# Value projections interleaved by weight chunk, squares and a norm row issued later, and a cross-attention regrouped through DRAM

## The chip, the cores and the metric

The kernel runs on one core of a Trainium2 chip. The metric is device time in microseconds (us) of one execution; the median of several executions counts. One further execution is recorded by the hardware profiler, and all rows below come from that one.

## The reference

Two small transformer stacks run one after the other on a sequence of 512 tokens with 1024 features, in float32. What matters here:

```python
# first_block, two layers; per layer
u = einsum('bsd,dc->bsc', rmsnorm(x), w_in)            # all projections
ya = forgetting_attention(qa, ka, va, log_f)           # 4 heads of 64
yb = dilated_mixture_attention(rope(qb), rope(kb), vb) # 6 heads of 64
yc = banded_attention(rope(qc), rope(kc), vc, 127, sinks)
x = x + (sigmoid(ga)*(ya*silu(za)) @ w_br_a + ... ) @ w_out

# second_block, two layers
h = h + even_mixer(...)       # layer 0: a = softmax(q1 k1) - lam * softmax(q2 k2), then a @ v,
                              # an rms norm of each head, and a pooling branch
h = h + cross_attention(...)  # q from h, k and v from a 256-token memory, 4 heads of 256, softmax, no mask
h = h + sq_relu_mlp(...)
# layer 1: a short convolution instead of the even mixer, then the same two
```

## The kernel before

Every matrix product of float32 operands is made of three TensorE products: each operand is split into a rounded high part and the rest, and high·high, high·low and low·high are added in one PSUM bank. Weights come in chunks of 128 x 1024 from DRAM into `raw` (4 slots). For each chunk ScalarE writes the high part `whi` (`round_hi`, 4 slots) and VectorE the rest `wlo` (`rest_lo`, 3 slots). `ahead(i)` issues these when the program comes to chunk i: high parts up to chunk i+3, rests up to i+2, each only if the slot's former user is done. `fetch(j + 4)` follows `rest_lo(j)` on the queue of SyncE (SP).

`gemm_fm` makes a product with features on the partitions (8 steps of 3 matmuls of 512 columns, lines 378 to 380). `gemm_tm` makes a value projection with tokens on the partitions: two chunks `w[0]` and `w[1]` hold the 1024 input features, and for each of two token tiles of one bank all 8 feature blocks k are added (lines 404 to 406, 256 columns each); it yields after every second k. `w[1]` holds k = 4 to 7.

Each engine runs its instructions in the order of the program. The program is written as Python generators: `drive(main, fill, num, den)` takes one step of the attention (`main`), then num/den steps of projections (`fill`), so that TensorE has projections to do while VectorE and ScalarE work at the softmax. `later(f, n)` puts f off to the n-th `flush()`; `flush` is called after each yield of an attention and at each end of a product (`finish`). `stage` puts three steps of a norm's column and row onto ticks (k steps) of the products that follow, and products that end before the last step is out hold their evacuation back (`held_back`).

In the first block, attention goes by units (a pair of heads with one or two query tiles). After the softmax its probabilities have to be transposed. Here (`by_dma=True`) ScalarE writes them, scaled, in blocks of 32 columns into `blocks`; `send_away` writes that to DRAM (`far`), and reads it back with the 32-row groups exchanged (4 DMAs, `grouped`); `turn_near` transposes 32 x 32 blocks on VectorE (`turned`). Step i holds `values` of unit i-3, `turn_near` of i-2, `scores` of i, a yield, `norm` and `send_away` of i, a yield.

The even mixer of the second block uses the same function without DMAs. `norm` takes the reciprocal of the sums, scales the first map by a `tensor_scalar` on VectorE, and adds the second map with a `scalar_tensor_tensor` (line 184). `turn` transposes on TensorE (line 705) and copies to `PTb` on ScalarE; `values` (line 729) reads that. After the last unit of a head, `head_done` copies the head out of PSUM on VectorE (line 1433), squares it on ScalarE and, three flushes later, sums the squares (`stats`).

The cross-attention (`cross`) runs in both layers. Step i holds `norm` of unit i-1 (a `tensor_tensor` over 512 columns), `scores` of i (line 1505, 8 matmuls), a yield, `values` of i-2 (line 1555), `turn` of i-1 (4 transposes of 128 x 128 on TensorE, line 1531, and a copy on ScalarE), a yield. In layer 0, five steps of projections stand at each yield, among them the keys and values of layer 1.

Of the kernel before, what the change touches and what calls it, by code (L numbers as in the profile page):

```python
# [7 lines left out]
ACT = mybir.ActivationFunctionType  # L8
ALU = mybir.AluOpType
# [133 lines left out]
def lay_out(nc, A, plan, T):  # L143
# [42 lines left out]
    def ts(o, a, s1, s2, f, g=ALU.bypass):  # L186
        return lambda e: e.tensor_scalar(o, a, s1, s2, f, g)  # L187
# [202 lines left out]
    def gemm_tm(src, chunks, evac, nt=4):  # L390

        w = [Weight(c) for c in chunks]
        for t0 in range(0, nt, 2):
            bank, free = G.take()
            o = None
            for t in (t0, t0 + 1):
                for k in range(8):
                    v, b = w[k // 4], 2 * (k % 4)
                    wh, wl = v.hi(b, 2), v.lo(b, 2)
                    xh, xl = src.hi[:, k, 128 * t:128 * t + 128], src.lo[:, k, 128 * t:128 * t + 128]  # L400

# [162 lines left out]
        return make  # L564


    def attention(units, done_pair, late_values=False, by_dma=False):

        st = {}
# [49 lines left out]
        def norm(u):  # L619
# [6 lines left out]
            if by_dma:  # L626
# [10 lines left out]
                    TB.give(t, last[-1])  # L637
                    o += last
                STT.give(s, o[-1])
                u["far"] = far, o  # L640
                return
            for j, (t, _) in enumerate(u["T"]):
                c = 12 + 2 * j
# [13 lines left out]
        def send_away(u):  # L657

            n = 2 * (u["cols"] // 128)
            src, o = u["far"]  # L660
            w, k = moved[0] % 2, moved[0] // 2
            moved[0] += 1
            far = A["far"][w][:, :, 0:32 * n]

            def write():
                u["out"] = Q.dma(SP, lambda e: e.dma_start(far.rearrange("j p c -> p j c"),
                                                           src[:, 0:128 * n].rearrange("p (j c) -> p j c", j=4)),
                                 T["s_t"][w], 16 * (k + 1), o, back[w])
                blocks.give(src, u["out"])
                later(rest)  # L670

            def rest():
                dst, dfree = grouped.take()
                for j in range(4):
                    landed = Q.dma(SP, lambda e, j=j: e.dma_start(
                        dst[32 * j:32 * j + 32, 0:128 * n].rearrange("p (i c) -> p i c", i=4),
                        far[j].rearrange("(i a) c -> a i c", i=4)),
                        T["s_u"][w], 16 * (4 * k + j + 1), u["out"], dfree)
                back[w] = landed
                u["near"] = dst, landed  # L680

            later(write)

        def turn_near(u):

            n = 2 * (u["cols"] // 128)
            src, landed = u["near"]
            dst, dfree = turned.take()
            o = op(DV, lambda e: e.transpose(dst[:, 0:128 * n].rearrange("p (k i b) -> p k i b", i=4, b=32),
                                             src[:, 0:128 * n].rearrange("p (i k b) -> p k i b", i=4, b=32)),  # L690
                   landed, dfree)
            grouped.give(src, o)
            u["PT"] = [o]
            u["cut"] = [lambda k, h=h: dst[:, u["cols"] * h + k:u["cols"] * h + k + 128] for h in range(2)]
            u["held"] = dst

        def turn(u):
            cols = u["cols"]
# [49 lines left out]
        if by_dma:  # L748
            for i in range(n + 3):
# [212 lines left out]
    for l in range(2):  # L962
# [167 lines left out]
            assert len(grouped.idle) == 1  # L1130
            drain()

        phase("forget", tok, 2, qA, kA, vA, [0, 1], [0, 1], gens_B(tokB), 90, 15, M[:, 4:6, :])
        phase("mix", tokB, 3, qB, kB, vB, [2, 3, 4], [2, 3, 4], gens_C(tokC), 138, 21, QKV[:, 4:6, :])
        phase("sink", tokC, 3, qC, kC, vC, [5, 0, 1], [0, 1, 2], gens_D(), 112, 15, QKV[:, 6:8, :])
# [295 lines left out]
    def head_done(u, banks, p):  # L1431
        h = u["pair"]
        o = op(DV, lambda e: e.tensor_copy(qE[:, h, :], banks[0]), p)
        t, sq = tmp_act_square(qE[:, h, :], o)

        def rest():
            hs[h] = stats(t, sq, out=lp[:, 136 + 4 * h:140 + 4 * h], inv=1.0 / 128)
            TMP.give(t, hs[h])

        later(rest, 3)  # L1440
        return [o]

    def even_main():
# [31 lines left out]

    run(mixed("ab_w_out", 0, halves(0), 1.0, "xa0", P1))
    row_end()

    def cross(l, gname):
        qX = E3[:, 0:8, :]  # L1480
# [37 lines left out]
        def norm(u):  # L1518
            t, s = u["t"], u["s"]
            r = op(DV, lambda e: e.reciprocal(s[:, 6:8], s[:, 4:6]), u["exp"])  # L1520
            u["P"] = op(DV, mult(both(t), both(t), s[:, 6:8].unsqueeze(2).broadcast_to([128, 2, 256])), r)
            STT.give(s, u["P"])

# [19 lines left out]

        def values(u):
            h, n = u["head"], u["half"]
            pt, ready = u["PT"]
# [13 lines left out]
            PTS.give(pt, p)  # L1560
            u["over"] = True
            if n == 1:
                for d in range(2):
# [5 lines left out]

        def main():  # L1570
            n = len(un)
            for i in range(n + 2):
                if 1 <= i <= n:
                    norm(un[i - 1])
# [6 lines left out]
                if 1 <= i <= n:  # L1581
                    turn(un[i - 1])
                yield

        def nxt(m, o):
            norm_tile(m, o, gname, P0, sqa)
# [144 lines left out]
    flush()  # L1731
    run(mixed("conv_w_out", 0, halves(0), 1.0, "xa1", P1))
    row_end()
    cross(1, "mlp1")

    end = [{"sum": None, "gained": []} for _ in range(2)]
# [270 lines left out]
```

How the kernel before makes its waits and increments, by code:

```python
    def dma(self, eng, fn, sem, val, *deps):  # L94
        self.op(eng, lambda e: fn(e).then_inc(sem, 16), *deps)
        return Landed(sem, val)
# [9 lines left out]
    def play(self, eng, e):  # L106
        seen = {}
        for o in self.of[eng]:
            need = {}
            for d in o.deps:
                v = need.get(id(d.sem), (0, None))[0]
                need[id(d.sem)] = (max(v, d.val), d.sem)
            for k, (v, s) in need.items():
                if seen.get(k, 0) < v:
                    e.wait_ge(s, v)
                    seen[k] = v
            ins = o.fn(e)
            if o.sig:
                ins.then_inc(o.sem, 1)
# [23 lines left out]
def lay_out(nc, A, plan, T):  # L143
# [1657 lines left out]
                o = send(0, *((0, 3), (3, 3), (6, 2))[m - 3])  # L1801
                if m == 5:
                    SB.give(end[0]["row"][0], o)
    mlp(1, n2)
    drain()
    last_norm(1)
    last_row(1)
    for m, n in ((0, 3), (3, 3), (6, 2)):
        send(1, m, n)
    op(SP, lambda e: e.wait_ge(T["s_o"], 16 * sent[0]))
    return Q, used
```

## Time and profile before

| | us |
|---|---|
| median of three executions | 2296.39 |
| lowest, highest | 2295.06, 2298.92 |
| profiled execution, its own time | 2297.81 |
| profiled execution, span from first to last instruction | 2296.0 |

TensorE is busy for 2274.3 us of the span, VectorE for 1286.3 us, ScalarE for 873.1 us. In the profile PE is TensorE's matmuls, PEld its weight loads, DVE is VectorE, ACT is ScalarE, POOL is GpSimd, SP is SyncE, whose queue issues the DMAs. A matmul's duration includes its way through the array; matmuls are pipelined, so that the distance between two starts, and not the duration, is what one takes from the engine.

### The profile page before, as it was taken

The numbers are of one execution on the slowest core, as the hardware profiler recorded it, in microseconds if no ns is written. First come the engines' busy times: TensorE is split into PE (matmuls) and PEld (weight loads), VectorE is DVE, ScalarE is ACT, GpSimd is POOL, SyncE is SP. The second block draws the span as 40 slices with busy tenths as digits, with TensorE's granted clock in tenths as the row PEclk, the third lists the DMA queues.
The fourth block names the chain that finished last, engine by engine and source line by source line (L and its number), as shares of the span: only waits on it lengthen the run. The fifth ranks groups of instructions, "written<-read, shape, count | busy, mean of one in ns | idle before, by whom it ended". The sixth has DMA issues, their size and how long they took to land.

```text
span 2296.0 us, 28246 instructions
## 1 busy us (share of the span) xinstructions
PE 2274.3 (99%) x11210; PEld 1853.2 (81%) x11210; DVE 1286.3 (56%) x2131; ACT 873.1 (38%) x1463; POOL 13.9 (1%) x14
## 2 busy tenths in 40 slices
PE   9999999999999999999999999999999999999998
PEld 7787778877777888788898888888888888888887
DVE  5856565566656556576555544444755536444445
ACT  5444443343445344254343422322322334332233
POOL 0000000000000000200000000000000000000000
PEclk9999999999999999999999999999999999999999
DMA  5655443335545333323224232222222213232231
GB/s 176 174 151 167 138 133 106 101 100 161 182 139 153 108 101 119 106 83 129 83 92 129 92 101 93 92 100 93 92 96 97 84 45 101 92 100 93 92 99 58
DMA packets 113640, 255.46 MB, mean 111 GB/s; under 512 B 11839, under 2 KB 57535, under 8 KB 113380
## 3 DMA queue, kind: packets, MB, share of 16 engines
q1 hardware_dynamic: 113508, 253.64, 35.0%
q8 instruction: 89, 1.46, 0.3%
q14 instruction: 43, 0.35, 0.1%
HBM read 227.64 MB, written 22.03 MB: 109 GB/s over the span
## 4 chain that ended last, share of the span: by engine, by line
PE 94%; DVE 3%; DMA 1%; ACT 1%; issue 1%; SPq 0%; POOL 0%; POOLq 0%; DVEq 0%; ACTq 0%
PE ps L378 27%; PE ps L380 27%; PE ps L379 27%; PE ps L729 2%; PE ps L581 2%; PE ps L404 2%; PE ps L405 2%; PE ps L406 2%; PE ps L1555 1%; PE ps L1505 1%; PE ps L470 1%; DMA t_PTX<-far 0%; POOL t_UP L178 0%; DMA far<-t_Tb 0%; DVE t_wlo L181 0%
## 5 line engine op out<-in xcount | busy, mean ns | idle before, releaser
L378 PE MATMUL ps<-t_P0H,t_whi 128*128 128x512 f32 x1664 | 669.1, 402 | 1.5 <-ACT t_P0H L190 1.2
L380 PE MATMUL ps<-t_P0H,t_wlo 128*128 128x512 f32 x1664 | 656.4, 395 | 0.0
L379 PE MATMUL ps<-t_P0L,t_whi 128*128 128x512 f32 x1664 | 655.3, 394 | 0.0
L190 ACT ACTIVATE t_whi<-t_raw 128x1024 fp32r<-128x1024 f32 (+3 forms) x395 | 404.4, 1028 | 395.7 <-PE ps L380 323.1
L181 DVE TENSOR_TENSOR t_wlo<-t_raw,t_whi 128x1024 fp32r<-128x1024 f32 (+3 forms) x394 | 467.9, 1188 | 38.1 <-PE ps L406 21.7
L378 PEld LDWEIGHTS ps<-t_P0H,t_whi 128*128 128x128 f32 x1664 | 313.8, 189 | 95.3 <-issue 20.6
L380 PEld LDWEIGHTS ps<-t_P0H,t_wlo 128*128 128x128 f32 x1664 | 313.0, 188 | 72.5
L379 PEld LDWEIGHTS ps<-t_P0L,t_whi 128*128 128x128 f32 x1664 | 313.4, 188 | 70.8 <-issue 2.4
L378 PE MATMUL ps<-t_P1H,t_whi 128*128 128x512 f32 (+1 forms) x932 | 361.5, 388 | 0.3 <-DVE t_P1L L181 0.3
L379 PE MATMUL ps<-t_P1L,t_whi 128*128 128x512 f32 (+1 forms) x932 | 359.7, 386 | 0.0
L380 PE MATMUL ps<-t_P1H,t_wlo 128*128 128x512 f32 (+1 forms) x916 | 355.7, 388 | 0.0
L378 PEld LDWEIGHTS ps<-t_P1H,t_whi 128*128 128x128 f32 x932 | 175.7, 188 | 38.6 <-DVE t_P1L L181 1.0
L379 PEld LDWEIGHTS ps<-t_P1L,t_whi 128*128 128x128 f32 x932 | 175.5, 188 | 37.3
L380 PEld LDWEIGHTS ps<-t_P1H,t_wlo 128*128 128x128 f32 x916 | 172.3, 188 | 37.8
L178 DVE TENSOR_TENSOR t_X<-ps,t_X 128x512 f32<-128x512 f32 (+1 forms) x136 | 89.7, 659 | 159.4 <-PE ps L380 159.4
L190 ACT ACTIVATE t_TMP<-t_TMP 128x512 f32<-128x512 f32 x89 | 56.3, 633 | 293.4 <-DVE t_TMP L184 229.3
L190 ACT ACTIVATE t_Tb<-t_Tb,t_ST 128x256 f32<-128x256 f32 (+3 forms) x160 | 83.1, 533 | 176.6 <-DVE t_ST L187 149.2
L184 DVE SCALAR_TENSOR_TENSOR t_TMP<-ps,t_RB 128x512 f32<-128x512 f32 x64 | 44.2, 691 | 178.4 <-PE ps L380 178.3
L190 ACT ACTIVATE t_P0H<-t_X,t_gv 128x512 fp32r<-128x512 f32 x56 | 40.5, 725 | 137.3 <-DVE t_X L184 124.5
L184 DVE SCALAR_TENSOR_TENSOR t_X<-ps,t_X 128x512 f32<-128x512 f32 x48 | 33.1, 691 | 100.3 <-PE ps L380 100.3
L190 ACT ACTIVATE t_P1H<-t_TMP 128x512 fp32r<-128x512 f32 x84 | 53.1, 633 | 83.2 <-DVE t_TMP L175 47.7
L181 DVE TENSOR_TENSOR t_P1L<-t_TMP,t_P1H 128x512 fp32r<-128x512 f32 x84 | 58.1, 691 | 23.0 <-ACT t_P1H L190 23.0
(241 smaller groups left out, 2342.3 us busy)
## 6 DMA issues: line engine op xcount, KB each, us to landing
t_raw<-in_wts SPq DMA_DIRECT2D x362, 512.0 KB, 3.5
far<-t_Tb SPq DMA_DIRECT2D x26, 384.0 KB, 3.3
far<-t_Tb SPq DMA_DIRECT2D x16, 512.0 KB, 3.0
t_PTX<-far SPq DMA_DIRECT2D x64, 96.0 KB, 2.3
t_raw<-in_wts SPq DMA_DIRECT2D x16, 384.0 KB, 3.1
t_QKV<-far SPq DMA_DIRECT2D x32, 128.0 KB, 3.4
t_raw<-in_wts SPq DMA_DIRECT2D x13, 256.0 KB, 3.0
t_PTX<-far SPq DMA_DIRECT2D x24, 128.0 KB, 4.1
```

Of the source, the lines that this page charges most:

```text
L178: return lambda e: e.tensor_tensor(o, a, b, ALU.add)
L181: return lambda e: e.tensor_tensor(o, a, b, ALU.subtract)
L184: return lambda e: e.scalar_tensor_tensor(out=o, in0=a, scalar=s, in1=b, op0=f, op1=g)
L190: return lambda e: e.activation(o, a, f, **k)
L378: e.matmul(bank[:, 0:N], wh, xh, start=first, stop=False)
L379: e.matmul(bank[:, 0:N], wh, xl, start=False, stop=False)
L380: return e.matmul(bank[:, 0:N], wl, xh, start=False, stop=end)
L404: e.matmul(out, xh, wh, start=k == 0, stop=False)
L405: e.matmul(out, xh, wl, start=False, stop=False)
L406: return e.matmul(out, xl, wh, start=False, stop=k == 7)
L581: i = e.matmul(bank[:, o:o + n], l, r, start=True, stop=True)
L729: i = e.matmul(held[b][0][base:base + rows, 128 * q:128 * q + 128], vs[k][j], cut[m](o + 128 * j), start=j == 0, stop=j == n // 128 - 1)
```

## The change

Four parts.

1. `gemm_tm` goes by weight chunk: for k = 0 to 3 both token tiles of a bank, then for k = 4 to 7 both. Only the first matmul of a bank starts its accumulation and only the last one stops it.
2. In the attention by DMA, one yield and flush more stands at step i = n, ahead of the `turn_near` of the last unit; the three phases have one main step more in the ratio (15 to 16, 21 to 22, 15 to 16), so that a main step has somewhat fewer projection steps.
3. In the even mixer, the first map is scaled on ScalarE (an `activation` with Copy) in place of VectorE, and the square of a head is put off by one flush, with the sum at the same flush as before. The third step of the stage at the second block's beginning (the norm's row) goes from tick 15 to tick 18.
4. In the cross-attention of layer 0, `norm` becomes two scaled copies on ScalarE into a block layout, issued one half step after the unit's scores; the probabilities go through DRAM as in the first block (`send_away`, `turn_near`, moved out of `attention`); `turn`, with its transposes and its copy, is gone there. The buffers are free pieces of the even mixer's tile and `PTb`; the PSUM bank of the transposes goes to the scores. Layer 1 keeps the old path.

```diff
@@ gemm_tm
-            for t in (t0, t0 + 1):
-                for k in range(8):
+            for n in (0, 4):
+                for t, k in ((t, k) for t in (t0, t0 + 1) for k in range(n, n + 4)):
...
-                        e.matmul(out, xh, wh, start=k == 0, stop=False)
+                        e.matmul(out, xh, wh, start=k == 0 and t == t0, stop=False)
...
-                        return e.matmul(out, xl, wh, start=False, stop=k == 7)
+                        return e.matmul(out, xl, wh, start=False, stop=k == 7 and t == t0 + 1)
@@ attention: norm, not by DMA
-                    o = [op(DV, ts(t[:, o:o + n], t[:, o:o + n], s[:, c + k:c + k + 1], None, ALU.mult), r)
+                    o = [op(AC, act(t[:, o:o + n], t[:, o:o + n], ACT.Copy, scale=s[:, c + k:c + k + 1]), r)
@@ attention: main loop by DMA
-                if i <= n:
+                for _ in range(0 if i > n else 2 if i == n else 1):
                     yield
                     flush()
@@ phases
-        phase("forget", ..., 90, 15, ...)   phase("mix", ..., 138, 21, ...)   phase("sink", ..., 112, 15, ...)
+        phase("forget", ..., 90, 16, ...)   phase("mix", ..., 138, 22, ...)   phase("sink", ..., 112, 16, ...)
@@ second block, norm row
-    stage((6, one), (12, two), (15, three))
+    stage((6, one), (12, two), (18, three))
@@ head_done
-        t, sq = tmp_act_square(qE[:, h, :], o)
-        def rest(): ...
-        later(rest, 3)
+        def square():
+            t, sq = tmp_act_square(qE[:, h, :], o)
+            def rest(): ...
+            later(rest, 2)
+        later(square)
@@ before cross(0)
+    blocks.idle = [(E3[:, 9, :], None)]
+    grouped.idle = [(E3[:, i, :], None) for i in (10, 11)]
+    turned.idle = [(ap, f) for ap, f in PTS.idle]
+    SB.idle += PTP.idle
+    PTP.idle = []
@@ cross: norm (the old one stays as norm_here for layer 1)
+            far, free = blocks.take()
+            f5 = far[:, 0:512].rearrange("p (j k a b) -> p a k j b", j=4, k=2, a=2)
+            o = [op(AC, act(f5[:, a], t[:, 256 * a:256 * a + 256].rearrange("p (k j b) -> p k j b", k=2, j=4),
+                            ACT.Copy, scale=s[:, 6 + a:7 + a]), r, free) for a in range(2)]
@@ cross: main, layer 0
+            for i in range(n + 2):
+                if i >= 2:
+                    turn_near(un[i - 2])
+                if i < n:
+                    scores(un[i])
+                yield
+                flush()
+                if i >= 2:
+                    values(un[i - 2])
+                if i < n:
+                    norm(un[i])
+                    send_away(un[i])
+                yield
+                flush()
```

## Rows read from the trace of the kernel before

**Rows 1.** The page: busy us of each engine, share of the span, instructions.
```profile
PE 2274.3 (99%) x11210; PEld 1853.2 (81%) x11210; DVE 1286.3 (56%) x2131; ACT 873.1 (38%) x1463; POOL 13.9 (1%) x14
```

**Rows 2.** The waits of TensorE: us in total, times, longest us.
```profile
PE ps L404 <- DVE t_wlo L181: 6.0, 4, 3.0
PE ps L729 <- ACT t_PTb L190: 2.4, 1, 2.4
PE ps L705 <- DVE t_Tb L184: 1.7, 3, 0.8
```

**Rows 3.** Timeline, TensorE at the two long waits of the value projections (start, duration).
```profile
103.28 0.39 PE L404 MATMUL ps<-t_whi,t_P0H 128*128 128x256 f32 x1 [1.78 <-DVE t_wlo L181]
103.50 0.28 PE L405 MATMUL ps<-t_wlo,t_P0H 128*128 128x256 f32 x1
103.62 0.28 PE L406 MATMUL ps<-t_whi,t_P0L 128*128 128x256 f32 x1
...
537.62 0.47 PE L404 MATMUL ps<-t_whi,t_P0H 128*128 128x256 f32 x1 [3.02 <-DVE t_wlo L181]
```

**Rows 4.** Timeline, VectorE ahead of the first of them.
```profile
95.79 1.25 DVE L689 STREAM_TRANSPOSE t_PTb<-t_PTX 128x1024 f32<-128x1024 f32 x1 [2.50 <-DMA t_PTX<-far]
...
102.01 1.22 DVE L181 TENSOR_TENSOR t_wlo<-t_raw,t_whi 128x1024 fp32r<-128x1024 f32 x1
```

**Rows 5.** Windows of TensorE: us, busy (instructions), granted clock, DMA share, GB/s.
```profile
104.00:108.00 4.00, 4.00 (x29) 0.57 0.70 167
```

**Rows 6.** The chain that ended last: start, us, what; 16 matmuls after each wait, undisturbed.
```profile
105.41 1.91 PE ps L729 x16
...
131.37 1.02 PE ps L729 x16
...
540.45 1.40 PE ps L729 x16
```

**Rows 7.** Timeline, TensorE at the second block's norm rows.
```profile
892.94 1.13 PE L470 MATMUL ps<-t_TMP,t_ones 128*128 128x512 f32 x2 [0.99 <-DVE t_TMP L175]
```

**Rows 8.** Timeline around the longest wait of the even mixer, several engines.
```profile
985.86 0.40 PE L380 MATMUL ps<-t_P0H,t_wlo 128*128 128x512 f32 x1
...
987.63 0.63 ACT L190 ACTIVATE t_TMP<-t_E 128x512 f32<-128x512 f32 x1 [1.87 <-DVE t_E L1433]
987.72 0.42 DVE L187 TENSOR_SCALAR t_Tb<-t_Tb,t_ST 128x384 f32<-128x384 f32 x1
...
988.17 0.47 ACT L190 ACTIVATE t_PTb<-ps 128x384 f32<-128x384 f32 x1
988.31 0.62 DVE L184 SCALAR_TENSOR_TENSOR t_Tb<-t_Tb,t_ST 128x384 f32<-128x384 f32 x1
988.69 1.65 PE L729 MATMUL ps<-t_PTb,t_E 128*128 128x128 f32 x6 [2.43 <-ACT t_PTb L190]
```

**Rows 9.** A ScalarE group by shape, 960 to 1060 us: busy us, mean ns.
```profile
L190 ACT ACTIVATE t_Tb<-t_Tb,t_ST 128x384 f32<-128x384 f32 x8 | 4.9, 617 | 9.9 <-DVE t_ST L187 9.9
```

**Rows 10.** Timeline, TensorE around one unit's transposes in the cross-attention of layer 0.
```profile
1132.62 0.39 PE L379 MATMUL ps<-t_P0L,t_whi 128*128 128x512 f32 x1
1132.86 0.39 PE L380 MATMUL ps<-t_P0H,t_wlo 128*128 128x512 f32 x1
1133.08 0.60 PE L1531 MATMUL ps<-t_ident,t_Tb 128*128 128x128 f32 x4
...
1133.76 0.40 PE L379 MATMUL ps<-t_P0L,t_whi 128*128 128x512 f32 x1
```

**Rows 11.** The chain that ended last: scores of two units in that attention.
```profile
1137.18 1.73 PE ps L1505 x8
...
1148.01 1.73 PE ps L1505 x8
```

**Rows 12.** DMA issues of the whole kernel: count, KB each, median us to landing.
```profile
far<-t_Tb SPq DMA_DIRECT2D x26, 384.0 KB, 3.3
...
t_PTX<-far SPq DMA_DIRECT2D x64, 96.0 KB, 2.3
```

More of the change, by code:

```diff
@@ L564, in residual, with send_away, write, rest @@
         return make
+    def send_away(u):
+        n = u["tiles"]
+        src, o = u["far"]
+        w, k = moved[0] % 2, moved[0] // 2
+        moved[0] += 1
+        far = A["far"][w][:, :, 0:32 * n]
+        def write():
+            u["out"] = Q.dma(SP, lambda e: e.dma_start(far.rearrange("j p c -> p j c"),
+                                                       src[:, 0:128 * n].rearrange("p (j c) -> p j c", j=4)),
+                             T["s_t"][w], 16 * (k + 1), o, back[w])
+            blocks.give(src, u["out"])
+            later(rest)
+        def rest():
+            dst, dfree = grouped.take()
+            for j in range(4):
+                landed = Q.dma(SP, lambda e, j=j: e.dma_start(
+                    dst[32 * j:32 * j + 32, 0:128 * n].rearrange("p (i c) -> p i c", i=4),
+                    far[j].rearrange("(i a) c -> a i c", i=4)),
+                    T["s_u"][w], 16 * (4 * k + j + 1), u["out"], dfree)
+            back[w] = landed
+            u["near"] = dst, landed
+        later(write)
+    def turn_near(u):
+        n = u["tiles"]
+        src, landed = u["near"]
+        dst, dfree = turned.take()
+        o = op(DV, lambda e: e.transpose(dst[:, 0:128 * n].rearrange("p (k i b) -> p k i b", i=4, b=32),
+                                         src[:, 0:128 * n].rearrange("p (i k b) -> p k i b", i=4, b=32)),
+               landed, dfree)
+        grouped.give(src, o)
+        u["PT"] = [o]
+        u["cut"] = [lambda k, h=h: dst[:, 64 * n * h + k:64 * n * h + k + 128] for h in range(2)]
+        u["held"] = dst
     def attention(units, done_pair, late_values=False, by_dma=False):
@@ L639, in norm @@
                 STT.give(s, o[-1])
-                u["far"] = far, o
+                u["far"], u["tiles"] = (far, o), 2 * kh
                 return
@@ L655, in norm @@
             STT.give(s, o[-1])
[L657 to L695, printed above, removed]
         def turn(u):
@@ L1433, in head_done, with rest @@
         o = op(DV, lambda e: e.tensor_copy(qE[:, h, :], banks[0]), p)
-        t, sq = tmp_act_square(qE[:, h, :], o)
-        def rest():
-            hs[h] = stats(t, sq, out=lp[:, 136 + 4 * h:140 + 4 * h], inv=1.0 / 128)
-            TMP.give(t, hs[h])
-        later(rest, 3)
+        def square():
+            t, sq = tmp_act_square(qE[:, h, :], o)
+            def rest():
+                hs[h] = stats(t, sq, out=lp[:, 136 + 4 * h:140 + 4 * h], inv=1.0 / 128)
+                TMP.give(t, hs[h])
+            later(rest, 2)
+        later(square)
         return [o]
@@ L1520, in norm, with norm_here @@
             r = op(DV, lambda e: e.reciprocal(s[:, 6:8], s[:, 4:6]), u["exp"])
+            far, free = blocks.take()
+            f5 = far[:, 0:512].rearrange("p (j k a b) -> p a k j b", j=4, k=2, a=2)
+            o = [op(AC, act(f5[:, a], t[:, 256 * a:256 * a + 256].rearrange("p (k j b) -> p k j b", k=2, j=4),
+                            ACT.Copy, scale=s[:, 6 + a:7 + a]), r, free) for a in range(2)]
+            STT.give(s, o[-1])
+            TB.give(t, o[-1])
+            u["far"], u["tiles"] = (far, o), 4
+        def norm_here(u):
+            t, s = u["t"], u["s"]
+            r = op(DV, lambda e: e.reciprocal(s[:, 6:8], s[:, 4:6]), u["exp"])
             u["P"] = op(DV, mult(both(t), both(t), s[:, 6:8].unsqueeze(2).broadcast_to([128, 2, 256])), r)
@@ L1545, in values @@
             h, n = u["head"], u["half"]
-            pt, ready = u["PT"]
+            pt, ready = (u["held"], u["PT"]) if l == 0 else u["PT"]
             if n == 0:
@@ L1559, in values @@
                    [x[1] for x in held[h]] if n == 0 else None)
-            PTS.give(pt, p)
+            (turned if l == 0 else PTS).give(pt, p)
             u["over"] = True
@@ L1571, in main @@
             n = len(un)
+            if l == 1:
+                for i in range(n + 2):
+                    if 1 <= i <= n:
+                        norm_here(un[i - 1])
+                    if i < n:
[4 more added lines that the diff above has]
+                        values(un[i - 2])
+                    if 1 <= i <= n:
+                        turn(un[i - 1])
+                    yield
+                return
             for i in range(n + 2):
-                if 1 <= i <= n:
-                    norm(un[i - 1])
+                if i >= 2:
+                    turn_near(un[i - 2])
                 if i < n:
@@ L1580, in main @@
                     values(un[i - 2])
-                if 1 <= i <= n:
-                    turn(un[i - 1])
+                if i < n:
+                    norm(un[i])
+                    send_away(un[i])
                 yield
+                flush()
         def nxt(m, o):
@@ L1733, in lay_out @@
     row_end()
+    PTS.idle, SB.idle, PTP.idle = turned.idle, SB.idle[1:], SB.idle[:1]
+    assert len(SB.idle) == 2
     cross(1, "mlp1")
```

6 lines of the change are left out of this document (3 added, 3 removed).

## Prediction

> **What bounds the kernel now.** I read the page first: TensorE is busy for 2274.3 of 2296.0 us [rows 1], so that time comes only from what TensorE does itself, from its idle time (21.7 us), and from its clock. Its list of waits [rows 2] shows where the idle time can be got: 6.0 us in four waits of the value projections (line 404) for a low part of a weight, 2.4 us in one wait of the even mixer's values (line 729), 1.7 us in three waits of its transposes (line 705). What is left is the start, the end, and a wait of 0.99 us at a norm row [rows 7]. VectorE and ScalarE have slack on average; they matter only where their order makes something late. The timeline around each wait says what came last, and the windows say what a wait costs beyond itself: after the first long wait the granted clock of four microseconds is 0.57 [rows 5], that is, mostly the lower of its levels, 1.2 GHz.
>
> **Value projections by chunk.** Nothing is added or removed on TensorE: the same matmuls in another order. The two long waits are 1.78 and 3.02 us [rows 3], the two short ones the rest of 6.0, 1.2 us. All four stand where the first matmul needs `w[1]`, after 12 matmuls with `w[0]`; now it comes after 24. A start follows the last by 0.12 us [rows 3], so the need comes 12 x 0.115 = 1.4 us later. By that alone 1.78 + 3.02 + 1.2 become 0.4 + 1.6 + 0: 4.0 us gained, the lower bound. The upper bound is 6.0. I take 6.0, because of the second edit here. The low part is late since VectorE stood for 2.50 us at a `turn_near` whose DMA had not landed, then did a unit's scores, and came to the weight at 102.01 [rows 4]. With 16 main steps for 90 projection steps in place of 15, the steps at the attention's ninth yield end with step 50, not 54. K's third product (steps 48 to 55) then fills the tenth yield alone, and the value projection (from step 56) starts only behind the next `values` and `scores`; before, its first four steps ran at the tenth. The low part is issued at the same place of the attention, behind unit 4's scores. From there TensorE asks for it 3 steps (6 matmuls of 256 columns or 3 of 512, 0.7 us each), some 2 us of attention matmuls and 1.4 us later than before: 5.5 us, more than the longest wait. The short waits belong to the second value projection, whose `w[1]` can only be split when the first one ends; there a `turn_near` stood ahead on VectorE. 1.4 us covers each of the two.
>
> With the waits goes the slow clock behind them. The 16 matmuls of `values` took 1.91 and 1.40 us after the waits and 1.02 undisturbed [rows 6]; that is 0.9 and 0.4 us, and the matmuls of 256 columns beside them stand at twice their distance. By the window, 4 us at 0.57 is 1.7 us lost [rows 5]; the other place, with 1.2 us from its twelve matmuls and 0.4 from `values`, is about the same. I take 3.3 us for both; 0 if a wait of about the first one's length stays.
>
> **Other main steps.** The extra yield issues nothing. It lets the last unit's DMA have one main step more. What covers the thinner filling is the three units in flight between scores and values: the trace has no wait of TensorE in these phases outside the four above. Cost 0; if that cover were gone, it would be waits at line 729, of the kind of the 2.4 us one [rows 2].
>
> **Norm row at tick 18.** The wait of 0.99 us is that of the next `spread_it` (the row `hrow`): its diagonal stands on VectorE behind two held-back evacuations, which wait for the norm row. With the row at tick 18 the diagonal is issued ahead of them. Gain 1.0 us. Late next are the two evacuations, by three ticks; the third product has the third bank, and the fourth starts 6 ticks later. Cost 0.
>
> **Even mixer.** At 986.26 TensorE is ready for unit 3's values and starts them at 988.69 [rows 8]. `PTb` was copied at 988.17 only because ScalarE, free since 985.76, stood at the square of the head, which waited for VectorE's copy of it. With the square behind, `PTb` is there at 985.76 + 0.5 = 986.3, and the wait is gone. But unit 4's transposes follow six matmuls of 128 columns later (0.7 us, at 0.11 each as in [rows 10]) and need the `scalar_tensor_tensor` that ended at 988.93 [rows 8]. So the wait moves: about 2 us remain at line 705. And this chain gets longer: the scaling took 0.42 us on VectorE [rows 8] and takes 0.62 on ScalarE [rows 9], with a crossing there and back (0.05 us each, as from 988.17 + 0.47 to 988.69). VectorE cannot use the time, since its next instruction waits for that copy. So 0.2 to 0.3 us more at each of the waits of line 705; twelve units have this chain, three waited. Net: 0.7 gained at the long wait, less 0.4 at the others: 0.3. Bounds: the long wait goes with its slow clock (2.4, and 1.6 as at each of the other two places: 4.0 gained), or ScalarE's queue makes each of the twelve copies later by half a copy more, 12 x 0.3 = 4 lost.
>
> **Cross-attention of layer 0.** Gone from TensorE: 4 transposes of 128 x 128 for each of 8 units. Their price is read from starts [rows 10]. Undisturbed starts stand 0.24 us apart (1132.62, 1132.86), so the second one after 1132.86 would be at 1133.32; it is at 1133.76. That is 0.44 us a unit, 8 x 0.44 = 3.5 us. (The Trainium skill, TensorE: Matmul & The Clock Gate, Part 4: PE-mode transpose, gives about 275 ns for one in a kernel. The trace differs where they follow each other: four of them span 0.60 us from the first start to the last end. By the page 32 would give 8.8 us, and the sum 2278.4.)
>
> Added: two scaled copies a unit on ScalarE (256 columns; at most 0.62 us each, as 384 take [rows 9]) for one copy of 512; on VectorE a `transpose` of 512 columns (1.25 us for 1024 [rows 4], so about 0.7) for a multiplication over the same 512; five DMAs on SP. Their latency is covered as follows. Units follow at 10.8 us [rows 11]. From `norm` to `turn_near` of a unit there are one half step and a whole one, some 14 us, and to its values on TensorE some 19. In that time: copies 1.2, writing 3.3, reading 2.3 from the last of four issues [rows 12], `turn_near` 0.7, and up to 3.5 (five steps) for each of the two flushes that issue them: 14.5 and the issues, if nothing overlaps. So VectorE may stand a little, and TensorE not. SP's weight loads queue behind its wait for the write, at most those 3.3 us; a weight is loaded three chunks ahead, and a chunk is 24 matmuls, 2.8 us at the least [rows 3], so over 8 us. Cost 0; from some 4 us later on, each microsecond costs 8.
>
> **The sum.** 6.0 + 3.3 + 1.0 + 0.3 + 3.5 = 14.1 us off the profiled execution's 2297.81: 2283.7. Its time is 1.4 above the median shown, so a median may come out at 2282.3; I say 2283.
>
> **Rivals.**
> *The waits at line 404 only get shorter.* If the low part moves with the attention, 4.0 is gained and the slow clock stays after waits of 0.4 and 1.6 us. For it: VectorE's standing at the DMA [rows 4] depends on SP's order, which shifts too. Gain 4.0 + 1.0 + 0.3 + 3.5 = 8.8: 2289. Chance 0.14.
> *The even mixer's wait really goes.* If VectorE's relief lets the chain start earlier, 4.0 in place of 0.3: 2297.8 - 17.8 = 2280. Against it: the busy chain up to 988.93. Chance 0.16.
> *ScalarE becomes the even mixer's bound.* 4 us lost there in place of 0.3 gained: 2288. Chance 0.07.
> *The regroup is late (slower).* Place: line 1555, waiting for `turn_near`. If the way through DRAM takes over 19 us, every unit waits; from 1.8 us each on it eats the 14.1. At 2.5 us each: 2297.8 - 14.1 + 20 = 2304. For it: VectorE did stand at such a landing, 2.50 us [rows 4]; against it: TensorE never did. (The Trainium skill, VectorE: DVE Perf Modes, Rules for kernel authors, tells to use TensorE for a 128 x 128 transpose where PSUM will do; this is the way in which it would be right here.) Chance 0.05.
> *It doesn't do what it says.* The waits come back elsewhere, worth as much as what went, within 4 us of 2296. Chance 0.06.
> The forecast has the rest, 0.52, and its own range is 2280 to 2287.
>
> **Chances and range.** The forecast and the three rivals with a gain hold 0.89: faster; the last rival is within 0.2% (4.6 us, about what a measurement of this kernel can tell): 0.06; slower 0.05. The range holds the forecast, the even mixer's two cases and the shortened waits, with a microsecond beyond: 2278 to 2290.
>
> **What would show it.** In the profile after: line 404 out of the list of TensorE's waits and clock 1.00 from 100 to 110 us; no wait of about 1 us near 892; line 1531 with 32 instructions, not 64, and no new wait at line 1555; the even mixer's wait at line 705, not 729, of about 2 us with a lower clock behind it. The prediction is wrong if line 404 still waits for over 1 us, if line 1555 waits for line 689, or if the even mixer's waits add up to much more or less than 4 us.

## The result, and the profile after

The changed kernel takes 2283.09 us (median of four executions, 2282.54 to 2284.20), the kernel before 2297.48 us in the same comparison: a ratio of 0.9939, with an interval of 0.9922 to 0.9956. The profiled execution took 2282.54 us with a span of 2280.8, 15.2 us shorter than before.

The page of the changed kernel, engines: TensorE is busy for 9.0 us less than in [rows 1], and its idle time fell from 21.7 to 15.5 us.

```profile
PE 2265.3 (99%) x11178; PEld 1844.8 (81%) x11178; DVE 1280.7 (56%) x2115; ACT 883.8 (39%) x1487; POOL 13.9 (1%) x14
```

The changed kernel, the waits of TensorE between 60 and 2200 us (total, times, longest), which answer to [rows 2]. Line 404 is gone from the list, and so is the norm row of [rows 7]; the even mixer's waits have changed places, from line 729 to line 705.

```profile
PE ps L705 <- DVE t_Tb L184: 4.2, 4, 2.0
PE ps L729 <- ACT t_PTb L190: 0.4, 1, 0.4
PE ps L378 <- DVE t_P1L L181: 0.3, 1, 0.3
```

Where the time came from is read best from starts: one and the same matmul is looked up in both timelines, and what it starts earlier was gained ahead of it. Between two such marks stands what one stage gave.

| the mark (TensorE) | before, us | after, us | earlier by | the stage ahead of it gave |
|---|---|---|---|---|
| first norm row of the first layer | 25.30 | 25.18 | 0.12 | |
| first norm row of the second layer | 452.24 | 447.59 | 4.65 | value projections, layer 1: 4.53 |
| last output projection of the first block | 875.23 | 864.83 | 10.40 | value projections, layer 2: 5.75 |
| memory's norm row | 916.75 | 905.14 | 11.61 | norm row of the second block: 1.2 |
| first head's norm row | 1045.40 | 1034.44 | 10.96 | even mixer: -0.65 |
| last values of the cross-attention, layer 0 | 1215.31 | 1200.65 | 14.66 | cross-attention: 3.70 |
| last norm row | 2288.92 | 2274.18 | 14.74 | all the rest: 0.1 |

The timeline of the changed kernel at the first value projection, which answers to [rows 3, 4]. VectorE stands at the transpose for 0.39 us, not 2.50, and has the low part at 100.3; TensorE now asks for it at 104.84, and the step from 104.73 to 104.84 is the usual one. From the scores of unit 4 (units are counted from 0) to this request there are 13.6 us now; before there were 8.1, from 93.44 to 101.50 (103.28 less the wait).

```profile
91.20 0.92 PE L621 MATMUL ps<-t_QKV 64*128 64x384 f32 x4
...
93.53 1.25 DVE L599 STREAM_TRANSPOSE t_PTb<-t_PTX 128x1024 f32<-128x1024 f32 x1 [0.39 <-DMA t_PTX<-far]
...
99.14 1.22 DVE L181 TENSOR_TENSOR t_wlo<-t_raw,t_whi 128x1024 fp32r<-128x1024 f32 x1
...
102.01 0.39 PE L404 MATMUL ps<-t_whi,t_P0H 128*128 128x256 f32 x1
...
104.73 0.28 PE L406 MATMUL ps<-t_whi,t_P0L 128*128 128x256 f32 x1
104.84 0.28 PE L404 MATMUL ps<-t_whi,t_P0H 128*128 128x256 f32 x1
```

The scores of unit 4 in the kernel before:

```profile
93.44 0.92 PE L581 MATMUL ps<-t_QKV 64*128 64x384 f32 x4
```

Windows of TensorE in the changed kernel (us, busy, granted clock, DMA share, GB/s), for the stretch of [rows 5] and for the even mixer's wait. The first is at the upper of the two levels, 2.4 GHz, now; the two windows around the wait at 978 are not: 5 x 0.19 + 5 x 0.15 = 1.7 us of clock are lost there.

```profile
104.00:108.00 4.00, 4.00 (x36) 1.00 0.51 167
...
975.00:980.00 5.00, 2.65 (x12) 0.81 0.65 210
980.00:985.00 5.00, 5.00 (x31) 0.85 0.00 0
```

The timeline around that wait, which answers to [rows 8]. `PTb` is copied early, as meant. But VectorE comes to the head's copy only at 976.09 and to the reciprocal at 976.70, ScalarE scales, VectorE adds, and the transposes of line 705 start 1.98 us late.

```profile
974.84 0.48 ACT L190 ACTIVATE t_PTb<-ps 128x384 f32<-128x384 f32 x1
...
975.37 0.94 PE L729 MATMUL ps<-t_PTb,t_E 128*128 128x128 f32 x6 [0.38 <-ACT t_PTb L190]
...
976.09 0.68 DVE L1433 COPY t_E<-ps 128x512 f32<-128x512 f32 x1
976.70 0.17 DVE L664 RECIPROCAL t_ST<-t_ST 128x4 f32<-128x4 f32 x1
...
976.90 0.61 ACT L190 ACTIVATE t_Tb<-t_Tb,t_ST 128x384 f32<-128x384 f32 x1 [1.58 <-DVE t_ST L664]
...
977.61 0.62 DVE L184 SCALAR_TENSOR_TENSOR t_Tb<-t_Tb,t_ST 128x384 f32<-128x384 f32 x1 [0.49 <-ACT t_Tb L190]
...
978.29 0.90 PE L705 MATMUL ps<-t_ident,t_Tb 128*128 128x128 f32 x3 [1.98 <-DVE t_Tb L184]
```

### The profile page after: what moved, and what is told of

Same layout as the page of the kernel before. It is cut to its first block, busy times and chain, and to the rows that moved or that the text cites. A ratio compares the mean times of both kernels' runs of the same rounds, so it can differ in the third digit from the quotient of the medians.

```text
span 2280.8 us, 28255 instructions
## 1 busy us (share of the span) xinstructions
PE 2265.3 (99%) x11178; PEld 1844.8 (81%) x11178; DVE 1280.7 (56%) x2115; ACT 883.8 (39%) x1487; POOL 13.9 (1%) x14
## 4 chain that ended last, share of the span: by engine, by line
PE 97%; DVE 1%; ACT 1%; POOL 0%; issue 0%; DMA 0%; SPq 0%; POOLq 0%; DVEq 0%; ACTq 0%
PE ps L378 28%; PE ps L380 27%; PE ps L379 27%; PE ps L621 2%; PE ps L729 2%; PE ps L404 2%; PE ps L405 2%; PE ps L406 2%; PE ps L1576 1%; PE ps L1515 1%; PE ps L470 1%; ACT t_Tb L190 1%; POOL t_UP L178 0%; PE ps L1013 0%; PE ps L1011 0%; PE ps L1012 0%
## 5 line engine op out<-in xcount | busy, mean ns | idle before, releaser
L190 ACT ACTIVATE t_Tb<-t_Tb,t_ST 128x256 f32<-128x256 f32 (+3 forms) x176 | 91.6, 534 | 149.6 <-DVE t_ST L187 125.8
L184 DVE SCALAR_TENSOR_TENSOR t_X<-ps,t_X 128x512 f32<-128x512 f32 x48 | 33.2, 691 | 100.3 <-PE ps L380 100.3
```

The source lines that it names most:

```text
L184: return lambda e: e.scalar_tensor_tensor(out=o, in0=a, scalar=s, in1=b, op0=f, op1=g)
L190: return lambda e: e.activation(o, a, f, **k)
```

## The experiments

All are timed in three rounds (the last in five) beside the kernel before. The columns "values" and "even" are the gains of these stages against the kernel before, read from starts as in the table above; what varies from execution to execution at the kernel's beginning is not in them (the first mark stands between 24.5 and 26.0 us). The intervals of the ratios overlap for most pairs of runs, so the readings below rest on the stages and on the lists of waits, not on differences of medians. The lists hold no wait below 0.15 us.

| run | median, us | ratio to before, interval | values 1, 2 | even |
|---|---|---|---|---|
| the change | 2283.09 | 0.9939 (0.9922 to 0.9956) | 4.5, 5.8 | -0.65 |
| e1 order as before | 2284.12 | 0.9948 (0.9931 to 0.9964) | 3.6, 5.1 | 0.80 |
| e2 ratios as before | 2285.27 | 0.9954 (0.9939 to 0.9969) | 4.3, 3.2 | 0.83 |
| e3 cross-attention on TensorE | 2286.48 | 0.9959 (0.9945 to 0.9974) | 4.5, 5.7 | -0.60 |
| e4 scaling on VectorE | 2280.84 | 0.9935 (0.9920 to 0.9950) | 4.5, 5.8 | 2.02 |
| e5 square as before | 2283.72 | 0.9936 (0.9920 to 0.9953) | 4.5, 5.8 | -0.96 |
| e6 regroup later | 2283.83 | 0.9934 (0.9919 to 0.9949) | 4.5, 5.7 | -0.72 |
| e7 chain earlier | 2281.61 | 0.9925 (0.9910 to 0.9940) | 4.5, 5.3 | 1.12 |
| e8 the same, VectorE | 2281.02 | 0.9923 (0.9908 to 0.9938) | 4.5, 5.8 | 2.04 |
| e9 short products apart | 2282.62 | 0.9942 (0.9927 to 0.9957) | 4.5, 5.5 | -0.06 |
| e10 the same, VectorE | 2280.57 | 0.9933 (0.9918 to 0.9948) | 4.5, 5.7 | 1.81 |
| e11 and chain earlier | 2280.21 | 0.9933 (0.9916 to 0.9949) | 4.5, 5.8 | 2.26 |
| e12 weight rests apart | 2279.35 | 0.9923 (0.9909 to 0.9936) | 4.5, 5.7 | 3.05 |

**e1: the old order of the value projections, the new ratios.**

```diff
-            for n in (0, 4):
-                for t, k in ((t, k) for t in (t0, t0 + 1) for k in range(n, n + 4)):
+            for t in (t0, t0 + 1):
+                for k in range(8):
...
```

> The changed kernel with the value projections in the old order (both halves of k for one token tile, then for the next); the new ratios and the extra yield stay. Theory of the prediction: the ratio alone already makes the demand for the second weight some 4 us later than before, more than the longest wait of 3.0 us, so neither long wait comes back and no slow clock; what the order still covers are the two short waits (0.6 us each), which come back: line 404 (402 here) waits 1.2 us in 2 places, +1.2 to +1.6 us, about 2284.5. Rival, the order is what removes them: all four waits come back, the long ones with slow clock behind, +4 us or more, 2287 and over.

The long waits stayed away. Two waits came back, both at the second value projection of a layer, 0.98 us in sum; the two stages lost 1.6 us together. First theory right, by size too. (The line kept its number.) The run keeps the new ratio and the extra yield together; the two were not undone one by one. The timeline of this run:

```profile
117.35 0.38 PE L404 MATMUL ps<-t_whi,t_P0H 128*128 128x256 f32 x1 [0.69 <-DVE t_wlo L181]
...
546.52 0.39 PE L404 MATMUL ps<-t_whi,t_P0H 128*128 128x256 f32 x1 [0.29 <-DVE t_wlo L181]
```

**e2: the new order, the old ratios and no extra yield.**

```diff
-                for _ in range(0 if i > n else 2 if i == n else 1):
+                if i <= n:
...
-        phase("forget", ..., 90, 16, ...)  # and 138, 22; 112, 16
+        phase("forget", ..., 90, 15, ...)  # and 138, 21; 112, 15
```

> The changed kernel with the old ratios (15, 21, 15) and without the extra yield; the value projections keep the new order. Theory of the prediction: the order alone makes the demand 1.4 us later, so the long waits of 1.78 and 3.02 us come back as 0.4 and 1.6 us, 2.0 us in sum; behind the second one at least the lower clock, 1.7 us: +2 to +5.5 us, 2285 to 2288.5. Rival, the order suffices and the ratio does nothing: line 404 does not wait, 2283. Second rival, the thinner filling costs something in the changed kernel: then this one is faster than 2283 outside of line 404.

Waits of 2.1 us came back, both in the second layer; that stage lost 2.5 us against the changed kernel, the first layer 0.3. No lower clock followed.

The sum is the 2.0 us of the first theory, but the places are not its places. The wait at 535.10 stands behind the first 24 matmuls of the first value projection: it is what is left of the 3.02 us, 0.58 and not 1.6. The wait at 549.11 stands behind 24 matmuls of the second one: there the kernel before waited for 0.58 us, and the new order was to cover that. And the first value projection of the first layer, where 0.4 us were expected, does not wait at all.

The reason for the first projections is in the timeline: the 24 matmuls with `w[0]` now fill the yield, and the attention's next `values` and `scores` come ahead of the request for `w[1]`. From unit 4's scores to the request there are 11.4 us in the first layer (94.17 to 105.60), 3.4 more than before, and not 1.4. At the second projection of the second layer TensorE asks at 547.62; VectorE has stood 1.03 us at a `turn_near` and starts the low part only at 547.87. So either edit alone takes most of the waits away, and only the two together take all.

The timeline of this run, TensorE and VectorE:

```profile
94.17 0.92 PE L621 MATMUL ps<-t_QKV 64*128 64x384 f32 x4
...
103.52 1.09 PE L729 MATMUL ps<-t_PTb,t_QKV 128*64 128x128 f32 x16
104.54 1.13 PE L621 MATMUL ps<-t_QKV 64*128 64x512 f32 x4
105.60 0.39 PE L404 MATMUL ps<-t_whi,t_P0H 128*128 128x256 f32 x1
...
535.10 0.39 PE L404 MATMUL ps<-t_whi,t_P0H 128*128 128x256 f32 x1 [0.58 <-DVE t_wlo L181]
...
546.97 0.98 DVE L599 STREAM_TRANSPOSE t_PTb<-t_PTX 128x768 f32<-128x768 f32 x1 [1.03 <-DMA t_PTX<-far]
547.87 1.18 DVE L181 TENSOR_TENSOR t_wlo<-t_raw,t_whi 128x1024 fp32r<-128x1024 f32 x1
...
549.11 0.39 PE L404 MATMUL ps<-t_whi,t_P0H 128*128 128x256 f32 x1 [1.49 <-DVE t_wlo L181]
```

**e3: the cross-attention of layer 0 as before.** The buffers' reassignment goes, and every place that chooses by layer takes the old path:

```diff
-            pt, ready = (u["held"], u["PT"]) if l == 0 else u["PT"]
+            pt, ready = u["PT"]
...
-            if l == 1:
+            if True:
                 for i in range(n + 2):
```

> The changed kernel with the cross-attention of layer 0 on the old path (its 32 transposes on TensorE, no way through DRAM). Theory: the gain of that part is the distance of the transposes on TensorE and nothing else, 8 units at 0.44 us = 3.5 us, lost again in that stage alone: 2286.6. Rival: the way through DRAM costs something elsewhere in the stage (weights late on SP's queue, VectorE standing at the landing), so that the loss is smaller than 3.5 us.

Measured +3.4 us in the median. Between the last two marks of the stage (1034.80 and 1204.71) it takes 169.91 us, as long as before, and 3.7 more than in the changed kernel; every other stage is as in the changed kernel. The gain of this part is the transposes alone, 3.70 / 32 = 0.116 us each. (The Trainium skill, TensorE: Matmul & The Clock Gate, Part 4: PE-mode transpose, gives about 275 ns for one of bf16 in a kernel. The trace agrees on the length: the float32 ones of the kernel before are listed at 0.27 us each on the mean of line 1531. But in [rows 10] they start 0.11 us apart, and what each takes from the engine is the 0.116 us.) The rule weighed in the prediction (the Trainium skill, VectorE: DVE Perf Modes, Rules for kernel authors) would have kept them on TensorE; where TensorE is what bounds the kernel and the data has time, the way round was the faster one by that much.

**e4: the scaling of the even mixer's first map on VectorE again.**

```diff
-                    o = [op(AC, act(t[:, o:o + n], t[:, o:o + n], ACT.Copy, scale=s[:, c + k:c + k + 1]), r)
+                    o = [op(DV, ts(t[:, o:o + n], t[:, o:o + n], s[:, c + k:c + k + 1], None, ALU.mult), r)
```

> The changed kernel with the scaling of the even mixer's first map back on VectorE; the square of a head stays late. Measured so far: this stage gained nothing, it lost 0.65 us in place of the 0.3 gained that was predicted. Theory: the scaling on ScalarE costs 0.2 us of duration and two crossings at each wait of line 705, so those waits shrink by 0.2 to 0.3 us each, some 1 us in sum: 2282. Rival: the loss comes from the square put off, or from what stands ahead on VectorE; then the waits of line 705 stay at 4.2 us and the time at 2283. Second rival: VectorE with the scaling is the slower one again, +0.5 us or more.

2.67 us better than the changed kernel in this stage: the waits add up to 3.6 us in place of 4.6, and no lower clock follows the longest of them. First theory right for the waits, which are 1.0 us shorter in sum; the rest, some 1.5 us, it did not have, and it is the clock's (see the last section). The waits of this run, and its window:

```profile
PE ps L705 <- DVE t_Tb L184: 3.6, 4, 1.9
```

```profile
975.00:980.00 5.00, 3.14 (x23) 1.00 0.61 197
```

**e5: the square of a head at once, as before; the scaling on ScalarE.** The diff is that of `head_done`, backwards.

> The changed kernel with the square of a head issued at once again; the scaling stays on ScalarE. The prediction said that putting the square off only moves the long wait (from line 729 to line 705). Theory: ScalarE then stands at the square until VectorE's copy of the head is there, copies PTb late, and scales the next unit behind that: the wait at line 729 comes back with about 2.4 us, the one at line 705 goes at this place, and the transposes start 0.5 to 1 us later than in the changed kernel; waits in sum 5 to 5.6 us in place of 4.6: 2283.6 to 2284. Rival, the square was the cause of that long wait and its move a real gain: in sum 6.5 us or more. The slow clock behind the wait may come or not, 1.7 us, and is told apart by the granted clock.

The long wait is back at line 729, the one at line 705 behind it is gone, and the waits add up to 5.1 us. With e4 all four corners are there (the corner of the kernel before lacks the other parts of the change too):

| sum of the even mixer's waits, us | scaling on VectorE | on ScalarE |
|---|---|---|
| square at once | 4.1 (before) | 5.1 (e5) |
| square one flush later | 3.6 (e4) | 4.6 (the change) |

The late square takes 0.5 us off (0.3 by starts, the changed kernel against e5), the scaling on ScalarE puts 1.0 us on, whatever the other is. The timeline of e5: the square waits for the head's copy, and the copy to `PTb` stands behind it, as in [rows 8].

```profile
977.07 0.63 ACT L190 ACTIVATE t_TMP<-t_E 128x512 f32<-128x512 f32 x1 [1.88 <-DVE t_E L1433]
977.60 0.47 ACT L190 ACTIVATE t_PTb<-ps 128x384 f32<-128x384 f32 x1
...
978.13 1.65 PE L729 MATMUL ps<-t_PTb,t_E 128*128 128x128 f32 x6 [2.88 <-ACT t_PTb L190]
979.57 0.85 PE L705 MATMUL ps<-t_ident,t_Tb 128*128 128x128 f32 x3
```

**e6: the write of the regrouping half a step later.**

```diff
-                    send_away(un[i])
+                    send_away(un[i], 2)      # later(write, 2) in place of later(write)
```

> The changed kernel with the two flushes of the cross-attention's regrouping made three: the write to DRAM is issued one half step later (5.4 us of the 10.8 us a unit), so the data is back that much later. The prediction said that TensorE has some 4 us of cover and each microsecond beyond costs 8: by that 8 x 1.4 = 11 us, 2294. Theory from the profile after: VectorE stands up to 5 us at each landing, but the values come on TensorE 9 us after the turn of VectorE, so 5.4 us are still covered, and the evacuations behind it have three banks: no more than 2 us, 2283 to 2285. Rival: VectorE's standing makes weights or evacuations late: waits at lines 378 or 404, +5 us or more.

No cost: the stage gives 3.71 us, the changed kernel's 3.70. VectorE now stands 12.7 us in four landings, TensorE never: its values start 4.8 us after the end of a transpose that had itself waited for 4.91. But the room is not the same at each unit: the transpose of the last one ends at 1200.74, 0.3 us ahead of its values. So a write 5.4 us later is covered, at the last unit only just.

```profile
1136.07 0.71 DVE L599 STREAM_TRANSPOSE t_PTb<-t_E 128x512 f32<-128x512 f32 x1 [4.91 <-DMA t_E<-far]
...
1141.57 1.89 PE L1576 MATMUL ps<-t_PTb,t_VM 128*128 128x256 f32 x8
...
1200.03 0.71 DVE L599 STREAM_TRANSPOSE t_PTb<-t_E 128x512 f32<-128x512 f32 x1 [3.48 <-DMA t_E<-far]
...
1201.05 1.89 PE L1576 MATMUL ps<-t_PTb,t_VM 128*128 128x256 f32 x8
```

**e7 and e8: the even mixer's chain half a step earlier**, in e8 with the scaling on VectorE as well.

```diff
-            if 1 <= i <= n:
-                norm(units[i - 1])
...
             if 1 <= i <= n:
                 turn(units[i - 1])
+            if i < n:
+                norm(units[i])
             yield
```

> The changed kernel with the scaling and adding of the even mixer's maps issued half a step earlier: behind the transposes of the unit before, in place of the beginning of the next step. Theory: what makes line 705 wait is not the length of this chain but that it stands on VectorE behind the evacuations and weight rests of half a step of filling; half a step earlier it is ready in time: line 705 stops waiting, 4.6 us and the slow clock behind go, about 1.7 us, and 0.2 us more at each of five waits: 2276 to 2277. Rival: VectorE then stands at the reciprocal until the exponentials of the same unit are done, and makes evacuations and weights late: new waits at line 378 or 404, less than 3 us gained or nothing.

> The same with the scaling back on VectorE as well. Theory: with the chain half a step earlier it has some 3 us of room, so that the engine of the scaling makes no difference (within 0.5 us of the run with the scaling on ScalarE): 2276. Rival: the 0.4 us more of VectorE per unit keep some waits of line 705: slower by 0.5 us or more; or the crossings still count: faster by 0.5 us or more.

The theory fell. Line 705 waits 2.0 to 2.3 us in place of 3.6 to 4.2, but a product's first step now waits for an evacuation that stands behind VectorE, and the sum is what it was: e8 gives 2.04 us in this stage, e4 2.02. e7's 1.12 against the changed kernel's -0.65 is the clock, which did not fall in it: its waits are 4.7 us against 4.6. The rival had it. (e7's 5.3 for the second layer's value projections has a wait of 0.22 us at line 404 in it, at the second projection: in the changed kernel the low part ends there at 545.51, and TensorE comes to it at 545.69.) The waits of e8:

```profile
PE ps L705 <- DVE t_Tb L184: 2.0, 2, 1.4
PE ps L378 <- DVE t_E L184: 1.7, 2, 1.1
```

**e9, e10, e11: the short products apart** (the four products of the pooling branch, one step each), with the scaling on ScalarE, on VectorE, and on VectorE with the chain earlier.

```diff
-        yield from queries(1)
...
-        for g in (0, 2):
-            yield from mix(w, g)
-            yield from mix(w, g + 1)
-            yield from queries(2 + g // 2)
+        for i in (1, 2):
+            q = queries(i)
+            for _ in range(4):
+                next(q)
+                yield
...
+            yield from mix(w, 2 * i - 2)
+            yield from q
+            yield from mix(w, 2 * i - 1)
+        yield from queries(3)
```

> The changed kernel with the four short products of the even mixer's filling (one step each, an evacuation on ScalarE and VectorE each) set four steps apart between the halves of two query projections, in place of two behind each other. Moving the chain earlier left a wait of 1.4 us at the same unit, since VectorE came to it only behind two of these evacuations (0.75 us each), two weight rests (1.22 each) and the head's copy. Theory: this pile is the cause of the long wait; apart, the wait of 2.0 us and the 0.4 us at line 729 before it go, with the slow clock behind (1.7 us); the other three waits of line 705 stay, some 2.2 us: 2278.5 to 2279. Rival: the weight rests and the head's copy alone are enough to make the unit late, or the pile only moves to another unit: waits in sum over 3.5 us, 2281 or more.

> The same, with the scaling on VectorE. Theory: the other waits of line 705 shrink by 0.2 us each besides: waits in sum some 1.5 us, 2278. Rival as for the run with the scaling on ScalarE; second rival, VectorE's 0.4 us more for each unit eat that: no faster than with ScalarE.

> The same as that, and the chain half a step earlier. Theory: with the pile gone the earlier chain is in time for every unit but the first, and the waits of a product's first step for an evacuation (1.7 us, behind VectorE's standing at the reciprocal) stay in part: waits in sum 1.5 to 2.5 us, 2278 to 2279, no better than without it. Rival: both moves add up, waits under 1 us: 2277.

This theory fell too. The wait at unit 4 stayed in all three (1.71, 1.59 and 1.59 us), and in e9 and e10 the first unit waited for 2.03 and 1.84 us where it had waited for 0.81 and 0.61. e11 shows what stands ahead of the unit's chain on VectorE, with the evacuations spread: two weight rests within 2.5 us (by the order of the program the pooling chunk ends one step behind the query projection's), the rest of a short product between them, and the head's copy.

```profile
971.91 1.22 DVE L181 TENSOR_TENSOR t_wlo<-t_raw,t_whi 128x1024 fp32r<-128x1024 f32 x1
973.70 0.75 DVE L184 SCALAR_TENSOR_TENSOR t_P1L<-ps,t_gv,t_P1H 128x512 fp32r<-128x512 f32 x1 [0.57 <-ACT t_P1H L190]
974.36 1.22 DVE L181 TENSOR_TENSOR t_wlo<-t_raw,t_whi 128x1024 fp32r<-128x1024 f32 x1
975.50 0.69 DVE L1438 COPY t_E<-ps 128x512 f32<-128x512 f32 x1
976.10 0.17 DVE L664 RECIPROCAL t_ST<-t_ST 128x4 f32<-128x4 f32 x1
```

**e12: the two chunks end four steps apart.** The third and fourth short product stand after the second and fourth step of the second query projection, so that the pooling chunk is done ahead of it; the rest is e11.

> The chain half a step earlier with the scaling on VectorE, and the four short products set so that their weight chunk is done four steps ahead of the query projection's, no longer one step behind it. With the products merely four steps apart the long wait had stayed (1.6 us at the same unit): VectorE's list there has two weight rests of 1.22 us within three microseconds, since two chunks end one step apart, and the unit's chain behind them. Theory: these two rests are the pile; apart by four steps, the wait of 1.6 us at line 705 goes or falls below 0.5, waits in sum under 1.2 us: 2278.5 to 2279. Rival: what makes the unit late is the crossing between VectorE and ScalarE ahead of it (rest of the short product behind the exponentials, head's copy), not the rests: the wait stays above 1 us, 2280.

The wait at unit 4 is gone, the list for line 705 holds 1.4 us (0.63 at the first unit, 0.74 at unit 3, where e11 did not wait), and the waits of this stage add up to 2.3 us: more than the 1.2 expected, but 2.3 less than in the changed kernel. By starts the stage gives 0.8 us more than e11, though the listed waits are only 0.4 shorter. Its 2279.35 us are the lowest median, 18.7 us under the kernel before in its own comparison (2298.06), though by the ratio it cannot be told from e7 and e8. The wait above 1 us that the rival forecast did not come, but its cause is not ruled out: together with the weight's rest, the rest of the short product (at 973.70 in e11, where VectorE also stood for 0.57 us) went from this place, and which of the two had made unit 4 late was not told apart. One weight rest is left ahead of the unit's chain, in the timeline of this run:

```profile
972.94 1.22 DVE L181 TENSOR_TENSOR t_wlo<-t_raw,t_whi 128x1024 fp32r<-128x1024 f32 x1
974.07 0.69 DVE L1443 COPY t_E<-ps 128x512 f32<-128x512 f32 x1
```

The waits of this run between 930 and 1070 us:

```profile
PE ps L705 <- DVE t_Tb L184: 1.4, 2, 0.7
PE ps L378 <- DVE t_P1L L184: 0.4, 1, 0.4
PE ps L378 <- DVE t_E L184: 0.3, 1, 0.3
PE ps L729 <- ACT t_PTb L190: 0.3, 1, 0.3
```

## Why the prediction was right, point by point

It said 2283, and 14.1 us off the profiled execution; the stages gave 14.5. That the sum came so near is partly luck: the value projections gave 1.0 us more than their terms, the norm row and the cross-attention 0.2 each, and the even mixer 0.95 less.

- *The waits of the value projections, 6.0, and the clock behind them, 3.3.* Right in place and mechanism: 10.3 us came. That the ratio (with the extra yield) removes the long waits alone was shown by e1, and the request that was to come 5.5 us later, counted from unit 4's scores, came 5.6 later (13.6 less 8.1). What the order does alone was worked out wrong, and its 4.0 us, measured as 3.9 in e2 (6.0 less 2.1), are luck: at the first projections it moves the request by 3.4 us, not 1.4, since `values` and `scores` get ahead of it, and at the second projection of the second layer 1.4 us did not cover the short wait, which grew to 1.49. The sum was 1.0 short. A listed wait counts from the modelled end of the matmul ahead, 0.28 us or more after its start, and undisturbed the next one would have started 0.12 us after that start [rows 3]; so each of four waits costs some 0.2 us more than its number. 2.4 + 0.4 + 1.7 = 4.5 for the first layer and 3.6 + 0.4 + 1.7 = 5.7 for the second are what the marks show.
- *The norm row, 1.0.* It gave 1.2, the same 0.2 more; in the timeline after, both rows stand without a wait. The tick alone was not undone in a run.

```profile
879.85 1.02 PE L470 MATMUL ps<-t_TMP,t_ones 128*128 128x512 f32 x2
881.40 1.02 PE L470 MATMUL ps<-t_TMP,t_ones 128*128 128x512 f32 x2
```

- *The even mixer, 0.3.* The term that failed, and in sign: -0.65. The wait moved from line 729 to line 705 with about 2 us left, as said, and with the lower clock behind it; that the clock fell is luck too, since in e1 and e2 the same wait was not followed by it. What was mis-sized are the two terms of the net: 0.7 for the square measured 0.5, and 0.4 for the longer chain on ScalarE measured 1.0 (e4, e5). The working counted the chain at three waits of line 705; it also made a fourth longer and left 0.4 us at line 729.
- *The cross-attention, 3.5.* It gave 3.70, all of it the distance of the transposes (e3). That the way through DRAM costs nothing was right; "from some 4 us later on, each microsecond costs 8" was wrong: it gives all eight units one and the same cover, and a write 5.4 us later lost nothing (e6). In the changed kernel the values start on TensorE between 1.0 and 9.3 us behind the end of VectorE's transpose, with the scores of another unit between (the unit below has the most). In the case of the 1.0 us VectorE did not wait for the data but came late itself, and there the later write changed nothing. At the last unit 3.4 us became 0.3. What eight late units would cost was not measured.

```profile
1131.16 0.71 DVE L599 STREAM_TRANSPOSE t_PTb<-t_E 128x512 f32<-128x512 f32 x1 [0.40 <-DMA t_E<-far]
...
1141.17 1.89 PE L1576 MATMUL ps<-t_PTb,t_VM 128*128 128x256 f32 x8
```

## What to carry to other kernels

Look up one and the same matmul in both timelines at each stage's end: the differences of starts give a budget by stage that mostly agrees from run to run within some hundredths of a microsecond, far finer than the medians. When a chain on the critical path crosses two engines, price a move by every wait that the chain feeds and by the queue that it joins on the other engine: 0.2 us of longer duration became 1.0 us here, at four waits of line 705 and one of line 729. And where one unit waits at the same place whatever is done to its own chain, list what stands ahead of it on the late engine. Here moving two short products, so that a weight's rest and an evacuation stood elsewhere on VectorE, took the wait away (0.8 us of the stage, e12 against e11), where moving the chain had given 0.0 (e8 against e4) and 0.4 us (e11 against e10). The products were not moved without the earlier chain.

## What was not expected of the hardware

The lower clock does not follow a wait by its length alone. In the changed kernel and in e1 the same instruction waits for the same 1.98 us at the same unit, ahead of the same work; in the one two windows of 5 us around it stand at 0.81 and 0.85, in the other at 1.00, and the stage differs by 1.45 us. In e2 the clock stayed up as in e1; in e3 and e6, with a wait of 1.98 and 1.99 us there, it fell. The waits of 1.78, 2.43 and 3.02 us of the kernel before were followed by the lower level, those of 1.84, 1.86 and 1.49 us in e10, e4 and e2 were not. What decides it stayed open; only one execution of each run was profiled, so that it may as well differ from execution to execution. For comparisons it means that 1.5 us between two variants may be the clock's alone: e4's 2.67 us are 1.2 of work and 1.5 of clock, and of the 3.7 us by which e12's stage is better than the changed kernel's, some 1.5 are. The windows of e1 around the wait:

```profile
975.00:980.00 5.00, 3.29 (x16) 1.00 0.38 111
980.00:985.00 5.00, 4.36 (x28) 1.00 0.30 98
```
